# Two attentions with their blocks of queries reversed, and the heads of one alternating between its groups

## The reference, cut to what matters

```
for layer in range(2):
    h = rmsnorm(x, norm1_g[layer]); proj = h @ w_in[layer]
    o_a = hgrn2(...)                       # first: a gated recurrence
    o_b = gate[0]*softmax(q.kc)vc          # second: 8 heads in 2 groups of 4,
        + gate[1]*softmax(q.ks, causal)vs  #   keys and values shared in a group
        + gate[2]*softmax(q.kw, causal)vw
    o_c = softmax(q.k/8 + cum_f[q] - cum_f[k], causal) v   # third: 4 heads
    x = x + concat(o_a, o_b, o_c) @ w_o[layer]
    x = x + relu(rmsnorm(x) @ w_up[layer])**2 @ w_down[layer]
```

## Time and profile before

| | us |
|---|---|
| median of three runs | 4534.27 (4531.8 to 4677.54) |
| profiled execution, first to last instruction (span) | 4523.3 |
| TensorE busy in it | 3919.6 (87%) |
| VectorE busy | 2430.4 (54%) |
| ScalarE busy | 1878.5 (42%) |
| DMA queue of the weights, share of 16 engines | 32.9% |

### The profile page before, as it was taken

How to read it: one execution, slowest core, us unless ns; L and a number is a source line. 1 busy time by engine, 2 the same in 40 slices (tenths; PEclk the granted TensorE clock), 3 DMA queues, 4 the chain that set the end, 5 groups by cost and what they waited for, 6 DMA issues and landing times. The chain is left out here.

```text
span 4523.3 us, 44200 instructions
## 1 busy us (share of the span) xinstructions
PE 3919.6 (87%) x17186; PEld 3121.6 (69%) x17187; DVE 2430.4 (54%) x3929; ACT 1878.5 (42%) x3023; POOL 149.1 (3%) x149
## 2 busy tenths in 40 slices
PE   6795998999897699889997685999986997799994
PEld 5685666787677666678775474888865766688883
DVE  3645324433365432343334445999974344799995
ACT  3201323323330032332324333888862342688884
POOL 0000000000000000000000001111100000111110
PEclk9855557999985555789998896999998998899997
DMA  3200001222120000122211013998872213589994
GB/s 127 57 19 19 1 1 38 75 93 93 57 75 20 19 1 1 38 75 93 92 65 42 19 47 135 377 368 358 353 295 98 81 42 123 197 358 360 368 368 163
DMA packets 139059, 588.79 MB, mean 130 GB/s; under 512 B 31296, under 2 KB 41024, under 8 KB 113120
## 3 DMA queue, kind: packets, MB, share of 16 engines
q1 hardware_dynamic: 119904, 569.08, 32.9%
q0 software_dynamic: 18944, 16.84, 1.1%
HBM read 596.32 MB, written 39.99 MB: 141 GB/s over the span
## 5 line engine op out<-in xcount | busy, mean ns | idle before, releaser
L179 PE MATMUL ps<-r,r 128*128 128x512 f32 (+1 forms) x10752 | 2549.2, 397 | 70.1 <-DVE r L705 30.5
L179 PEld LDWEIGHTS ps<-r,r 128*128 128x128 f32 x10752 | 2029.3, 192 | 539.9 <-issue 75.3
L2504 DVE TENSOR_TENSOR r<-mem,r 128x1024 fp32r<-128x1024 f32 x768 | 908.9, 1224 | 103.5 <-ACT r L2452 91.1
L2452 ACT ACTIVATE r<-mem 128x1024 fp32r<-128x1024 f32 x768 | 791.4, 1062 | 200.6 <-PE ps L179 174.3
L705 DVE TENSOR_TENSOR r<-mem,r 128x512 fp32r<-128x512 f32 (+1 forms) x512 | 340.2, 674 | 756.1 <-ACT r L687 755.4
L687 ACT ACTIVATE r<-mem 128x512 fp32r<-128x512 f32 (+1 forms) x512 | 311.8, 618 | 890.8 <-PE ps L179 890.8
L179 PE MATMUL ps<-mem 128*128 128x64 f32 (+7 forms) x2440 | 468.8, 351 | 24.1 <-DVE mem L2278 13.5
L179 PEld LDWEIGHTS ps<-mem 128*128 128x128 f32 (+1 forms) x2440 | 454.5, 276 | 38.7 <-issue 19.1
L1320 PE MATMUL ps<-mem 64*128 64x512 f32 (+4 forms) x512 | 325.5, 734 | 4.5 <-DVE mem L1479 1.6
L1372 DVE CUSTOM_DVE_ANT_0 mem<-ps,mem 128x512 f32<-128x512 f32 (+3 forms) x224 | 122.5, 549 | 365.8 <-PE ps L1320 304.3
L1349 ACT ACTIVATE mem<-mem 128x512 f32<-128x512 f32 (+3 forms) x224 | 135.9, 607 | 409.6 <-DVE mem L1372 409.3
(11 more groups left out here) (282 smaller groups left out, 2427.6 us busy)
## 6 DMA issues: line engine op xcount, KB each, us to landing
mem<-in_w_up SPq DMA_DIRECT2D x80, 2048.0 KB, 17.9
mem<-in_w_down SPq DMA_DIRECT2D x80, 2048.0 KB, 7.8
mem<-in_w_gate SPq DMA_DIRECT2D x64, 2048.0 KB, 12.9
mem<-in_w_in SPq DMA_DIRECT2D x12, 2048.0 KB, 7.8
mem<-in_odd_w_qkv SPq DMA_DIRECT2D x6, 2048.0 KB, 8.1
mem<-in_w_o SPq DMA_DIRECT2D x4, 2048.0 KB, 8.1
mem<-yd SPq DMA_DIRECT2D x8, 1024.0 KB, 8.8
mem<-in_rel SPq DMA_DIRECT2D x32, 224.0 KB, 3.6
```

What stands on the lines that cost most here:

```text
L179: r = e.matmul(out, a, b, start=start and i == 0, stop=stop and i == n - 1, skip_group_check=skip)
L2452: act.e.activation(wh, w, ACT.Copy).then_inc(*self.S["ex_wh"](self.l, e, i))
L2504: dve.e.tensor_tensor(wl, w, wh.bitcast(F32), SUB).then_inc(*self.S["ex_wl"](self.l, e, i))
```

## The change

The units of both stages are made in the order t = 3, 2, 1, 0, so that the blocks with 512 keys come first and those with 128 keys last. The number of a unit's group, and with it the output bank and the place of its sums, follows the new order; the closings and the bias compute t from it. In the second attention the heads go in the order 0, 4, 1, 5, 2, 6, 3, 7, so that the partitions of the score product's operands alternate. A head's place in the output bank stays `64 * h`, while its sum lies in unit order, so that the closing reads sums, gates and the bank through patterns with the group as a dimension of its own. Nothing is added to or taken out of the instructions of any engine.

```diff
+    HEADS = (0, 4, 1, 5, 2, 6, 3, 7)
 class Nsa, setup:
-        for t in range(4):
+        for t in (3, 2, 1, 0):
             for kind in range(2):
-                for h in range(8):
+                for h in self.HEADS:
                     gg = h // 4
...
-                                           lambda j, vc=vc: F.PJ[:, j, vc:vc + 64], 64, 2 * t + kind, 64 * h,
-                                           h == 0, h == 7))
+                                           lambda j, vc=vc: F.PJ[:, j, vc:vc + 64], 64, 2 * (3 - t) + kind, 64 * h,
+                                           h == self.HEADS[0], h == self.HEADS[-1]))
 class Nsa, finish:
-        S, v, (t, kind) = self.S, dve.e, divmod(g, 2)
+        S, v, (i, kind) = self.S, dve.e, divmod(g, 2)
+        t = 3 - i
...
-        dve.then("at_f", v.tensor_tensor(r, r, self.N.gs[:, t, 8 + 8 * kind:16 + 8 * kind], MUL))
-        tv = self.TMP.rearrange("p (h d) -> p h d", h=8)
-        dve.then("at_fin", v.tensor_tensor(tv, self.out(g)[:, :].rearrange("p (h d) -> p h d", h=8), bc(r, 2, 64), MUL),
-                 self.name, g)
+        rh = r.rearrange("p (i g) -> p i g", g=2)
+        dve.then("at_f", v.tensor_tensor(rh, rh, self.N.gs[:, t, 8 + 8 * kind:16 + 8 * kind].rearrange(
+            "p (g i) -> p i g", g=2), MUL))
+        tv = self.TMP.rearrange("p (g i d) -> p i g d", g=2, i=4)
+        dve.then("at_fin", v.tensor_tensor(tv, self.out(g)[:, :].rearrange("p (g i d) -> p i g d", g=2, i=4),
+                                           bc(rh, 3, 64), MUL), self.name, g)
 class Fox, setup:
-        for t in range(4):
+        for t in (3, 2, 1, 0):
...
-                                       K.cmask, lambda j, vc=vc: F.PJ[:, j, vc:vc + 64], 64, t, 64 * h, h == 0, h == 3))
+                                       K.cmask, lambda j, vc=vc: F.PJ[:, j, vc:vc + 64], 64, 3 - t, 64 * h, h == 0, h == 3))
 class Fox, bias:
-        t, h = divmod(u, 4)
+        i, h = divmod(u, 4)
+        t = 3 - i
 class Fox, finish:
-        dve.then("at_fin", v.tensor_tensor(self.F.MIX[:, g, 768:1024].rearrange("p (h d) -> p h d", h=4),
+        dve.then("at_fin", v.tensor_tensor(self.F.MIX[:, 3 - g, 768:1024].rearrange("p (h d) -> p h d", h=4),
```

## The result

The changed kernel took 4440.31 us (median of four runs, 4350.75 to 4477.4); the kernel before, over four runs of its own, 4605.91 (4531.8 to 4678.75). The ratio, worked out from the faster runs of each kernel, is 0.962, with a 95% interval of 0.953 to 0.972: faster. The forecast was 4350, its range 4315 to 4450. Runs of one and the same kernel differ by up to 147 us (before) and 127 us (after); that has a cause inside the program, to which the experiments come back, and it hides part of the size of the change.

What follows compares the result with a forecast made beforehand. TensorE at its lower clock was taken to bound the second and third attention streams: 2 x (114.6 + 31.5) = 292.2 in place of 476.5 us, so 4534.3 - 184.3 = 4350 us. Range 4315 to 4450.

Steps and rivals of the forecast that it cites:

- The bound and the mechanism: Second and third attention: TensorE bounds the streams at the lower clock; long units first keep the 2.4 GHz they begin with.
- The prices per unit: Attention units at 2.4 GHz: 2.48 us for 512 keys, 0.84 for 128; interpolated 1.93 for 384, 1.39 for 256.
- The second attention: Stream per layer: 92.8 us for long blocks, 19.9 for the 128-key block, 1.9 for the ends; 114.6 us.
- The closing's hole: 128-key block of the second attention: closings hold VectorE, TensorE stands still some 1.6 us, then the clock falls.
- The third attention: Stream per layer: 23.2 us for long units, 5.8 for the last four at 1.45, 2.5 for ends; 31.5 us.
- The base from which it was subtracted: Whole kernel before: the shown median, 4534.27 us, from which 184.3 us is taken; the profiled span was 4523.3.
- D: Odd, layer 2's sixteen-head attention, falls to the lower clock: 139 us more, 4685, or 4489 with A; 4%.
- A: Second and third attention gain as forecast: 4350 us for the kernel, own range 4315 to 4405; 66%.
- C: All four second and third attention streams fall in their start: 488 against 476.5 us, kernel 4546; 14%.
- B: Holds in part: clock falls after the first block (4447) or in one second attention's start (4428); 16%, centre 4430.
- Alternation and closing patterns: Second attention's alternating heads and four-dimensional closing patterns: each counted as 0; patterns at worst 11 us on VectorE.
- The rule weighed against the trace: Skill's rule that sustained activity lifts TensorE's clock would make unit order irrelevant; rejected since 67.60 us without gap stayed at 0.50.

Runs made afterwards that it cites:

- the filled kernel: Changed kernel with three unused products in Odd's preamble, plus one unused product before the transposes at units 54 and 62 of the second attention: 4322.65 us.

## Why the prediction was right, and where it was not

**The bound and the mechanism**: right for the two stages that the change touches. PE bounds the streams, the level of its clock is set by how a stream begins, and with long units at the front the second and third attention keep 2.4 GHz. The hole ahead of the stream undoes it, the alternation alone does not do it, and of two other orders the second attention came out as the theory has it. It is not the whole rule: that "which one it has is what it began with" fails for Odd, which in the changed kernel lost the clock within its first score products though the preamble ended at 1.00. And the 0.50 "for all that remains" is that of layer 0: in layer 1 of the kernel before, the clock came back 2.8 us before the end of the second attention and 2.9 us before that of the third.

**The prices per unit**: right to the hundredth. 512 and 128 keys stand 2.48 and 0.84 us apart; the interpolated 1.93 and 1.39 were also measured. The first four distances of a block are still longer (2.27 twice and 2.16 twice, then 1.93), since the transposes and value products between them belong in part to older units with more keys; that is some 1.1 us per block (2 x 0.34 + 2 x 0.23) which the sum did not have.

**The second attention**: forecast 114.6, measured 110.8 and 112.6. The closing's hole was 0.99 us of idle where 1.6 were counted, and the clock fell later, at unit 60 of layer 0 and at 57 of layer 1, than after the half of the block that the sum assumes. And the hole that the sum took for the cause ("after such a hole") is not needed: with it filled the fall still came in 2 of 5 streams.

**The third attention**: forecast 31.5, measured 26.9. The last four units did not fall (4 x 0.61 = 2.4), and what remains for the ends is 0.3 and not 2.5 us. The four streams: 292.2 forecast, 277.2 measured, 199.3 us saved in place of 184.3.

**The base from which it was subtracted** is the step that was off. The median of the runs shown, 4534.27, stood for the kernel before; but the times of that kernel scatter between two levels, and four runs give 4605.91, 71.6 more. (The 11.0 us between that median and the span are also mostly a difference between executions: the changed kernel's run of 4465.27 us has a span of 4463.9, 1.4 less.) The row for it was at hand: "the highest run shown, 4677.54, is 143 us above the median" stands in D, with 139 worked out as the price of Odd at the lower level. The price in D was right (Odd at 1.2 GHz costs 142.5 us). Its deciding point, whether the work just before Odd's first unit finds the clock up, was not: the clock was at 1.00 there in both profiles. Right again was "nothing in the change touches what happens there". The chance of 4% was not: it should have been that of any single execution, of both kernels. "With A, 4489" is what runs of 4465 and 4477 are. So it is by luck that the median of 4440 lies in the range: it falls between runs near the one level and runs near the other, for which the range did not allow. The 4350 is that of executions in which Odd holds, which the three unused products bring out: 4329.99 measured.

**C**, the fall in the start of all four streams, was not seen in the changed kernel; **B**, one of them, was seen in one profile of the kernel with the hole filled and the closing split (two of its four runs have the time for it), and in the order that begins with 256 keys. **Alternation and closing patterns**, counted at nothing: right for the alternation (4327.68 against 4329.99), and by DVE's busy time (56.82 us for 59.14) the patterns cost nothing either. The prediction counted up to 0.9 us of idle time in the start (0.79 measured) and had the saving right (0.86 us in 2.84, "between nothing and one 512-key product"). It did not put the two together: it is the alternation that makes the hole, which with straight heads is next to nothing. Whether that hole matters to the clock is not shown.

**The rule weighed against the trace**, that sustained activity lifts the clock: Odd after the change has PE busy for 302.30 of 302.30 us at 0.50 (3379.5 to 3681.8). The Trainium skill ("TensorE: Matmul & The Clock Gate", Part 1, What's actually happening) would have the clock up by then; here it was not, over the whole stage. The measurement decides. The clock can rise within a stream, though: at 558.1 us in the filled kernel, behind a dip of some 4 us, and in the kernel before at 1785.7, where PE had been busy for 184.30 of 184.30 us at 0.50.

**Open.** What decides about Odd's level when two executions show the same bursts and the same idle times. What the runs between the two levels are (4350.75 and 4415.35 of the changed kernel, 4560 to 4644 of the kernel before), for example whether Odd can change its level on the way; 4415 is where one second attention fallen in its start would put a run, 4330 + 83, but no profile caught it. Why the last block falls in some streams in which no hole is left. And whether the start's hole has a part in the fall in the start: two runs of twelve against none of ten is too few to tell.

## What to carry to other kernels

Where a stage is bound by TensorE, read the granted clock of its stream and of the few microseconds in which it begins; a stream that begins at the upper level with long units can keep it, though Odd lost it in six of eight profiles, and one that begins with short units can lose it for all but its last few us. At the lower level a stream took 1.7 to 1.9 times as long. Put the long units first and the short ones last, and try products that nobody reads in the idle times of TensorE ahead of a stream: three of them, 3 us of TensorE time, took a swing of 140 us out of every run. And when single runs of a kernel differ by more than a per cent or two, find the stage that has two lengths before subtracting anything from a median.

## What was not expected of the hardware

One and the same stream of instructions can have two lengths: 306.7 or 164.2 us for Odd in the kernels after and before, 191.5 or 112.7 for the second attention within one execution. No profile shows a length between; the times of unprofiled runs suggest that there are some. A stage can run for 302 us without a gap in TensorE's work and not get the upper level, and a stream can lose it with no gap before the fall. Two executions with idle times equal to the hundredth of a microsecond ahead of the stage came out at different levels. And a saving on TensorE (1.98 us for 2.84, score products on different halves of the rows) turned, at the one place where TensorE waits for another engine anyway, into idle time.
